# Opening of a two-layer diffusion step in two halves of the features, and its keys and values stored as soon as they are complete

## The chip, the core and the metric

The kernel runs on one core of one Trainium2 chip. Its engines are TensorE (PE in the profile, with PEld for the loading of weights), VectorE (DVE), ScalarE (ACT), GpSimd (POOL) and SyncE (SP); each runs its own stream of instructions in order, and they wait for each other on semaphores. Transfers are issued from the streams of SP, ACT and POOL. The metric is the device time in microseconds of one execution, median of several.

## What is computed

One inference step on 128 context tokens and 256 latent tokens (three tiles of 128 tokens, 1024 features, everything float32). Two layers, each a token mixer and then a mixture of experts; the first mixer is a gated linear recurrence (HGRN2), the second differential attention:

```python
for i in range(DEPTH):                                   # DEPTH = 2
    sh1, sc1, g1, sh2, sc2, g2 = split(silu(cond) @ w_ada[i] + b_ada[i], 6)
    h = rmsnorm(x, norm_g[i, 0]) * (1.0 + sc1) + sh1
    if i == 0:
        y, new_state = hgrn2_mixer(h, ...)               # q, inp, zf, zb, g = split(h @ w_in, 5)
    else:
        q, k, v = split(h @ w_qkv, 3); q, k = rmsnorm(q), rmsnorm(k)
        new_k, new_v = k, v                              # of the context tokens: outputs
        y = diff_attention(rotary(q), concat(rotary(k), cache_k), concat(v, cache_v)) @ w_out
    x = x + g1 * y
    h = rmsnorm(x, norm_g[i, 1]) * (1.0 + sc2) + sh2
    x = x + g2 * hier_moe(h, ...)                        # 16 experts, two for each token
```

`cond` is one vector for the context tokens and another for the latent ones. The shift `sh1` and the scale `sc1` have 1024 numbers each.

## The kernel before

Every engine's stream is written out by hand, in one function, `trunk`, with a block for each engine; nothing is scheduled by a tool. Weights stream from the chip's memory into a ring of eight slots of 2 MB (`ring`, `full`: it has landed, `used`: PE is done with it). SP issues them in the order in which its block names them, and waits for `used` before it fills a slot again.

**The opening.** `w_ada` comes in blocks of 512 columns, 2 MB each (`ada`). Blocks 0 and 1 are the shift, blocks 2 and 3 the scale; 0 and 2 belong to features 0 to 511 (k = 0 to 3 of eight groups of 128), 1 and 3 to features 512 to 1023 (k = 4 to 7). SP issues block 0, the tokens `x`, blocks 1 to 3, then the weights of head 0 (`head(0, 4, 0)`, four transfers of 512 KB), the masks and the states, head 1, and so on. On PE a block goes through 8 products with `cT` (`modulation_products`), ACT copies the result out of PSUM to `raw` (`raw_out`), PE turns it (`turn_rows`, 4 transposes), and DVE sums it into `adaln` (`block_columns`). When all four blocks are in, DVE makes `mod` (`columns`), and ACT and DVE write the modulated tokens `uT` (12 instructions each, `modulate`) from the tiles that PE has transposed before (`turn_tile`, 8 transposes for a tile). Then PE projects head 0: `proj(0, 0, 0, part)` for part 0 to 8. Parts 0, 2 and 4 are the products of q, zf and zb with features k = 0 to 3, parts 1, 3 and 5 those with k = 4 to 7 (4 products of 128x384 each), parts 6 to 8 the values (24 products of 128x128). Then `scan(0, ...)` starts; during the scan of one head PE projects the next. In the profile a product in float32 shows as two MATMUL records, so x8 there is 4 products.

**Keys and values.** In the second layer PE makes 18 products of `w_qkv` (b = 0 to 17: 0 to 5 queries, 6 to 11 keys, 12 to 17 values; b = 6 and 9 are the context keys, normalised into `AT["kp"]`, which lies in `xn[:, 1]`; b = 12 and 15 are the context values in `AT["v"][:, 0]`). ACT copies each out. After all 18 it issues the two stores `out["new_v"]` and `out["new_k"]`, 512 KB each, both counted by `at["out"]`. The attention then runs over 24 units (head, tile): for unit u PE makes the scores, DVE takes their maxima (`maxima`), ACT the exponentials, DVE the difference (`difference`), PE transposes and multiplies with the values, DVE writes the result into `xn[:, t]` (`attended`, u = 1 writes into tile 1, where the keys lie). Before the first maxima, DVE waits until both stores have landed:

```python
            dve.wait_ge(at["out"], 32)
            dve.wait_ge(at["ckT_ready"], 2)
            maxima(0)
```

In the attention PE also makes one block of the second layer's `w_ada` for every three units (`late_product`, 8 products, in line between the units), and the expert weights' slots come free as blocks, attention and output products end. Both expert stages stream 100 MB each through the ring.

Of the kernel before, what the change touches and what calls it, by code (L numbers as in the profile page):

```python
# [129 lines left out]
def trunk(nc, a, out):  # L130
    with ExitStack() as ctx:
# [45 lines left out]
        def down_rows(slot):  # L177
# [19 lines left out]
            mod_cols=("mod_cols", 0, 12), mod_ready=("mod_ready", 0, 2), diag=("diag", 0, 8),  # L197
# [40 lines left out]
        EARLY = 4  # L238

# [115 lines left out]
        def _(sp):  # L355
# [53 lines left out]
            ada(0, 0, 0, 0)  # L409
            sp.dma_start(x_rows[:, 0, :], a["x_prompt"][0]).then_inc(x_in, 16)  # L410
            sp.dma_start(x_rows[:, 1:3, :], a["x_sample"][0].rearrange("(t p) d -> p t d", p=P)).then_inc(x_in, 16)
            for blk in range(1, 4):
                ada(0, blk, blk, 0)
            head(0, 4, 0)
            sp.dma_start(masks[:, :, :].rearrange("p n t -> p (n t)"), a["const_mask"]).then_inc(heads_in, 16)
# [40 lines left out]
        def _(pe):  # L456
# [25 lines left out]
            def first_modulation(raw):  # L482

                ada_block(0, 0, 0)
                ada_block(1, 0, 1)
                first_turn(0, raw)
                need(pe, 0, "xn_ready", 1)
                turn_tile(0, "xT_done", xn, 0, (4, 5))
                ada_block(2, 0, 2)
                first_turn(1, raw)  # L490
                need(pe, 0, "xn_ready", 2)
                turn_tile(0, "xT_done", xn, 1, (0, 1))
                ada_block(3, 0, 3)
                first_turn(2, raw)
                first_turn(3, raw)
                need(pe, 0, "xn_ready", 3)
                turn_tile(0, "xT_done", xn, 2, (2, 3))

            def first_turn(blk, raw):
                if blk >= 2:  # L500
                    need(pe, 0, "mod_cols", blk - 1)
                turn_mod(0, blk, raw, blk % 2, 6 + blk % 2, blk + 1)
# [239 lines left out]
            first_modulation(raw)  # L742
# [112 lines left out]

            need(pe, 0, "uT_act", T)
            need(pe, 0, "uT_dve", T)
            for part in range(9):
                proj(0, 0, 0, part)
# [168 lines left out]
        def _(act):  # L1028
# [56 lines left out]
            def second_norm_end(n):  # L1085

                need(act, n, "mod_ready", 2)
# [74 lines left out]
            for blk in range(4):  # L1162
                raw_out(0, HG["raw"], blk % 2, blk, blk, 1, blk - 1 if blk >= 2 else None)
            need(act, 0, "mod_ready", 1)
            for t, src in enumerate((4, 0, 2)):
                modulate(0, "xT_done", "uT_act", t, src)
# [88 lines left out]
            need(act, 1, "mod_ready", 1)  # L1255
# [5 lines left out]
            for b in range(18):  # L1261
                act.wait_ge(at["proj"], b + 1)
                if b < 12:

                    if b >= 2:
                        act.wait_ge(at["turned"], b - 1)
                    A(AT["sq"][:, b % 2, :], bank[b % 2][:, :], ACT.Square).then_inc(at["squares"], 1)
                    act.wait_ge(at["meansq"], b + 1)
                    A(stat[:, 2, 0:8], stat[:, 1, 0:8], ACT.Sqrt).then_inc(at["root"], 1)
                else:  # L1270
                    half, t = divmod(b - 12, T)
                    A(AT["v"][:, t, 512 * half:512 * half + 512], bank[b % 2][:, :], ACT.Copy).then_inc(at["v_ready"], 1)
# [71 lines left out]
        def _(dve):  # L1344
# [29 lines left out]
            def columns(n, norm, first_part, blocks):  # L1374
# [5 lines left out]
                    .then_inc(S[n]["mod_ready"], 1)  # L1380
# [283 lines left out]
            for blk in range(4):  # L1664
                block_columns(0, blk, 6 + blk % 2, blk + 1)
            columns(0, 0, 0, 4)
            need(dve, 0, "mod_ready", 1)
            for t, src in enumerate((5, 1, 3)):
                modulate(0, "xT_done", "uT_dve", t, src)
# [114 lines left out]
            need(dve, 0, "mod_ready", 2)  # L1784
# [7 lines left out]
            columns(1, 0, 0, 4)  # L1792
# [6 lines left out]
            need(dve, 1, "mod_ready", 1)  # L1799
# [223 lines left out]
```

## Time and profile before

| | us |
|---|---|
| median of 3 runs | 1255.93 (1255.23 to 1256.7) |
| the profiled execution, its own time | 1257.95 |
| its span in the trace | 1256.1 |
| PE busy | 1122.5 (89% of the span) |
| DVE, ACT, POOL busy | 427.5, 226.4, 135.8 |
| moved by DMA | 317.08 MB, mean 252 GB/s |

The profiled execution is 2.02 us above the median of the runs, and 1.85 us longer than its span. All times of rows count from the start of the span.

### The profile page before, as it was taken

Reading aid. Unit: us, or ns where it says so; the run is one execution under the profiler, and the core shown is the slowest. Engines: PE = TensorE matmul, PEld = TensorE weight load, DVE = VectorE, ACT = ScalarE, POOL = GpSimd, SP = SyncE. Lnnn points to the kernel's source line nnn. Section 1 sums busy time; section 2 is a strip of 40 time slices with the busy share of each in tenths; the row PEclk is TensorE's granted clock in tenths of the full one; section 3 lists DMA queues with packets and bytes.
Section 4 is the critical chain, followed back from the end, with each engine's and each line's share of the span. In section 5 each row is a group of like instructions: output and inputs, shape, how many; then the busy total and the mean of one; then the engine's idle time right before and its main releaser. Section 6 shows DMA issues by size and latency. Waiting matters only on the chain.

```text
span 1256.1 us, 19811 instructions
## 1 busy us (share of the span) xinstructions
PE 1122.5 (89%) x8500; PEld 673.4 (54%) x8500; DVE 427.5 (34%) x1102; ACT 226.4 (18%) x527; POOL 135.8 (11%) x219
## 2 busy tenths in 40 slices
PE   4899999998899989999986799987989799999894
PEld 1566666665444566666653344434545656666551
DVE  1155555555522350000003755306853330000006
ACT  2201010111121321111000311115632211101010
POOL 0334333333100000000002100000000000000012
PEclk8899999999899989999998899998999699999897
DMA  9974444434923338999999913135761169999993
GB/s 347 272 237 135 136 136 135 135 135 160 373 109 129 134 132 325 427 424 425 424 426 409 342 67 134 67 133 199 262 244 67 69 268 403 426 425 425 426 423 151
DMA packets 97601, 317.08 MB, mean 252 GB/s; under 512 B 3792, under 2 KB 38912, under 8 KB 81120
## 3 DMA queue, kind: packets, MB, share of 16 engines
q1 hardware_dynamic: 90160, 298.05, 62.0%
q10 hardware_dynamic: 5248, 10.97, 2.2%
q0 software_dynamic: 2096, 6.67, 1.5%
q8 instruction: 72, 1.18, 0.4%
q14 instruction: 25, 0.20, 0.0%
HBM read 304.67 MB, written 11.01 MB: 251 GB/s over the span
## 4 chain that ended last, share of the span: by engine, by line
issue 70%; PE 20%; DMA 3%; DVE 3%; SPq 2%; POOL 1%; ACT 0%; POOLq 0%; DVEq 0%
PE bank L757 11%; PE bank L766 4%; DMA ring<-expert_rows,moe_row 2%; PE bank L782 2%; PE bank L468 1%; SPq L360 1%; SPq L372 1%; DVE ring L1632 1%; DMA ring<-in_w_ada 1%; DMA ring<-in_hgrn_w_in 1%; PE bank L838 1%; PE bank L791 0%; DVE hg_kf L1714 0%; DVE uT L1630 0%; PE bank L831 0%
## 5 line engine op out<-in xcount | busy, mean ns | idle before, releaser
L656 PE MATMUL bank<-ring,xn 128*64 128x256 f32 x1536 | 174.0, 384 | 12.0 <-DMA ring<-in_moe_w_up 7.9
L656 PEld LDWEIGHTS bank<-ring,xn 128*64 128x64 f32 x1536 | 110.8, 139 | 77.8 <-issue 11.2
L757 PE MATMUL bank<-uT,ring 128*128 128x384 f32 x384 | 137.6, 504 | 4.5 <-DMA ring<-in_hgrn_w_in 4.5
L945 PE MATMUL bank<-ring,uT 128*128 128x512 f32 x288 | 126.3, 593 | 1.3 <-issue 1.3
L1620 DVE TENSOR_TENSOR moe_hh<-xn,bank 128x256 f32<-128x256 f32 x32 | 13.5, 421 | 307.7 <-ACT xn L1125 307.6
L670 PE MATMUL bank<-ring,xn 128*64 128x512 f32 x384 | 88.4, 614 | 15.5 <-DMA ring<-in_moe_w_down 15.5
L645 PE MATMUL bank<-moe_g,moe_h 128*128 128x128 f32 x768 | 96.6, 285 | 2.4 <-DVE moe_g L1518 2.4
L645 PEld LDWEIGHTS bank<-moe_g,moe_h 128*128 128x128 f32 x768 | 92.6, 200 | 7.9 <-issue 7.9
L757 PEld LDWEIGHTS bank<-uT,ring 128*128 128x128 f32 x384 | 70.9, 193 | 47.1 <-ACT uT L1048 4.7
L1973 POOL TENSOR_TENSOR moe_flag<-con 128x1 f32<-128x1 f32 x2 | 0.4, 192 | 862.3 <-DMA expert_rows<-xn 862.3
L945 PEld LDWEIGHTS bank<-ring,uT 128*128 128x128 f32 x288 | 53.6, 190 | 65.1 <-issue 65.1
L574 PE MATMUL bank<-ring,uT 128*128 128x512 f32 x192 | 84.0, 593 | 0.8 <-ACT uT L1068 0.8
L670 PEld LDWEIGHTS bank<-ring,xn 128*64 128x64 f32 x384 | 28.7, 142 | 66.4 <-issue 65.4
L468 PE MATMUL bank<-ring,cT 128*32 128x512 f32 x384 | 53.2, 677 | 8.6 <-DMA ring<-in_w_ada 8.6
L1675 DVE COPY_PREDICATED hg_att<-masks,bank 128x384 f32<-128x384 uint8 x104 | 59.9, 576 | 0.0
L574 PEld LDWEIGHTS bank<-ring,uT 128*128 128x128 f32 x192 | 35.9, 190 | 43.0 <-issue 42.1
L656 PE MATMUL bank<-moe_ring,xn 128*64 128x256 f32 x512 | 57.2, 380 | 0.2 <-DMA moe_ring<-in_moe_w_up 0.2
L1125 ACT ACTIVATE xn<-bank 128x256 f32<-128x256 f32 x32 | 12.3, 383 | 205.2 <-PE bank L656 205.2
L656 PEld LDWEIGHTS bank<-moe_ring,xn 128*64 128x64 f32 x512 | 38.3, 137 | 20.1 <-issue 3.9
L766 PE MATMUL bank<-ring,uT 128*128 128x128 f32 x384 | 47.2, 277 | 0.0
L766 PEld LDWEIGHTS bank<-ring,uT 128*128 128x128 f32 x384 | 44.7, 192 | 0.6
L879 PE MATMUL bank<-ring,uT 128*128 128x512 f32 x96 | 42.2, 594 | 0.6 <-DVE adaln L1370 0.5
(261 smaller groups left out, 1262.7 us busy)
## 6 DMA issues: line engine op xcount, KB each, us to landing
ring<-in_w_ada SPq DMA_DIRECT2D x24, 2048.0 KB, 9.8
ring<-in_moe_w_gate SPq DMA_DIRECT2D x24, 2048.0 KB, 18.1
ring<-in_moe_w_up SPq DMA_DIRECT2D x24, 2048.0 KB, 22.3
ring<-in_moe_w_down SPq DMA_DIRECT2D x24, 2048.0 KB, 27.5
ring<-in_hgrn_w_in SPq DMA_DIRECT2D x32, 512.0 KB, 8.2
moe_ring<-in_moe_w_gate SPq DMA_DIRECT2D x8, 2048.0 KB, 22.5
moe_ring<-in_moe_w_up SPq DMA_DIRECT2D x8, 2048.0 KB, 24.2
moe_ring<-in_moe_w_down SPq DMA_DIRECT2D x8, 2048.0 KB, 21.2
```

The costliest lines, as they stand in the source:

```text
L468: last = mm(bank[to][32 * g:32 * g + 32, :], cT[:, 2 * g + r, :], cols(slot)[:, 2 * g + r, :], start=(r == 0), stop=(r == 1))
L574: last = mm(bank[4 + half][:, :], uT[:, k, t * P:(t + 1) * P], cols(slot)[:, k, :], start=(k == 0), stop=(k == KC - 1))
L645: last = mm(bank[half][:, k * P:(k + 1) * P], m["h"][:, t, (4 * half + k) * P:(4 * half + k + 1) * P], m["g"][:, t, :, :], start=(t == 0), ...
L656: last = mm(bank[2 + e][64 * g:64 * g + 64, 256 * part:256 * part + 256], m["xe"][:, k, 64 * e:64 * e + 64], cols(slot)[:, k, 256 * g:256 ...
L670: last = mm(bank[5 + 2 * half][64 * e:64 * e + 64, :], m["hT"][:, e, j, 64 * g:64 * g + 64], rows_of[e][:, g, j, 512 * half:512 * half + 512],
L757: last = mm(to[:, 0:TOK], w[:, k, f, :], uT[:, k, :], start=(k == 0), stop=(k == KC - 1))
L766: last = mm(bank[3][:, t * P:(t + 1) * P], uT[:, k, t * P:(t + 1) * P], w[:, k, 1, :], start=(k == 0), stop=(k == KC - 1))
L782: last = mm(to[g * size:(g + 1) * size, here], lhs[:, here], rhs[:, here], start=True, stop=True)
L879: last = mm(bank[4 + half][:, :], uT[:, k, t * P:(t + 1) * P], cols(2 + half)[:, k, :], start=(k == 0), stop=(k == KC - 1))
L945: last = mm(bank[b % 2][:, :], uT[:, k, t * P:(t + 1) * P], cols(slot)[:, k, :], start=(k == 0), stop=(k == KC - 1))
L1620: v.tensor_tensor(m["hh"][:, e, :], m["sg"][:, e, :], bank[2 + e][:, 256:512], ALU.mult)\
L1675: return v.copy_predicated(HG["att"][:, :].rearrange("p (t n) -> p t n", t=T), mask, src[:, 0:TOK].rearrange("p (t n) -> p t n", t=T))
```

## The change

Two independent places are changed.

First the opening. SP issues `x` first, then the blocks in the order 0, 2, head 0, 1, 3. PE, ACT and DVE finish the first half of the features (blocks 0 and 2, k = 0 to 3 of all three tiles) before the second. A block's products all go to bank 6 and its transposes to bank 7, so that a block waits for the copy of the one before (`mod_raw`). The transposes of `x` go by halves as well, into banks 3 to 5, those of the second half once the first half has been read. ACT modulates tile 0 and DVE tiles 1 and 2 of each half. PE makes parts 0 and 2 of head 0 with the first half of `uT`, then the blocks 1 and 3, then part 4, and the other six parts once the second half of `uT` is there. Counts of `mod_ready` go up by one everywhere behind it.

Second the stores. ACT issues `new_k` in the turn of b = 10 and `new_v` in that of b = 16; DVE waits for their landing not before the first maxima but before `attended(1)`.

```diff
+        FIRST_BLOCKS = (0, 2, 1, 3)
...
-            ada(0, 0, 0, 0)
             sp.dma_start(x_rows[:, 0, :], a["x_prompt"][0]).then_inc(x_in, 16)
             sp.dma_start(x_rows[:, 1:3, :], a["x_sample"][0].rearrange("(t p) d -> p t d", p=P)).then_inc(x_in, 16)
-            for blk in range(1, 4):
-                ada(0, blk, blk, 0)
+            ada(0, 0, 0, 0)
+            ada(0, 2, 2, 0)
             head(0, 4, 0)
+            ada(0, 1, 1, 0)
+            ada(0, 3, 3, 0)
...
+            def first_block(at, raw):
+
+                if at >= 1:
+                    need(pe, 0, "mod_raw", at)
+                ada_block(FIRST_BLOCKS[at], 0, 6)
+
+            def first_turn(at, raw):
+
+                if at >= 1:
+                    need(pe, 0, "mod_cols", at)
+                turn_mod(0, None, raw, at % 2, 7, at + 1)
+
+            def first_features(half):
+
+                for t in range(T):
+                    need(pe, 0, "xn_ready", t + 1)
+                    for j in range(4):
+                        k = 4 * half + j
+                        last = nc.tensor.transpose(bank[3 + t][:, j * P:(j + 1) * P], xn[:, t, k * P:(k + 1) * P], ident)
+                    last.then_inc(S[0]["xT_done"], 1)
...
-            first_modulation(raw)
+            first_block(0, raw)
+            first_turn(0, raw)
+            first_block(1, raw)
+            first_features(0)
+            first_turn(1, raw)
+            need(pe, 0, "uT_act", 1)
+            need(pe, 0, "uT_dve", 1)
+            first_features(1)
...
+            proj(0, 0, 0, 0)
+            proj(0, 0, 0, 2)
+            first_block(2, raw)
+            first_turn(2, raw)
+            first_block(3, raw)
+            first_turn(3, raw)
+            proj(0, 0, 0, 4)
             need(pe, 0, "uT_act", T)
             need(pe, 0, "uT_dve", T)
-            for part in range(9):
+            for part in (1, 3, 5, 6, 7, 8):
                 proj(0, 0, 0, part)
...
+                if b == 16:
+                    act.wait_ge(at["v_ready"], 4)
+                    act.dma_start(out["new_v"][0, 0].rearrange("p h d -> p (h d)"), AT["v"][:, 0, :]).then_inc(at["out"], 16)
...
-            act.wait_ge(at["v_ready"], 6)
-            act.dma_start(out["new_v"][0, 0].rearrange("p h d -> p (h d)"), AT["v"][:, 0, :]).then_inc(at["out"], 16)
-            act.dma_start(out["new_k"][0, 0].rearrange("p h c d -> p (h c d)"),
-                          AT["kp"][:, :, :].rearrange("p b n -> p (b n)")).then_inc(at["out"], 16)
+                if b == 10:
+                    act.wait_ge(at["normed"], 10)
+                    act.dma_start(out["new_k"][0, 0].rearrange("p h c d -> p (h c d)"),
+                                  AT["kp"][:, :, :].rearrange("p b n -> p (b n)")).then_inc(at["out"], 16)
...
-            dve.wait_ge(at["out"], 32)
             dve.wait_ge(at["ckT_ready"], 2)
             maxima(0)
             for u in range(len(units)):
                 if u + 1 < len(units):
                     maxima(u + 1)
                 difference(u)
+                if u == 2:
+                    dve.wait_ge(at["out"], 32)
                 if u >= 1:
                     attended(u - 1)
```

On PE, in the opening before (`bank<-ring,cT` are the products of a block of w_ada, `bank<-con,hg_raw` its transposes, `bank<-con,xn` the transposes of the tokens, `bank<-uT,ring` the projections):

```order
L468 MATMUL bank<-ring,cT 32x512 x16
L474 MATMUL bank<-con,hg_raw 128x128 x4
L560 MATMUL bank<-con,xn 128x128 x8
L468 MATMUL bank<-ring,cT 32x512 x8
L474 MATMUL bank<-con,hg_raw 128x128 x4
L560 MATMUL bank<-con,xn 128x128 x8
L468 MATMUL bank<-ring,cT 32x512 x8
L474 MATMUL bank<-con,hg_raw 128x128 x8
L560 MATMUL bank<-con,xn 128x128 x8
L757 MATMUL bank<-uT,ring 128x384 x24
L766 MATMUL bank<-ring,uT 128x128 x24
L773 MATMUL bank<-hg_q,hg_kd 128x128 x6
```

And the same place on PE after the change:

```order
L470 MATMUL bank<-ring,cT 32x512 x8
L476 MATMUL bank<-con,hg_raw 128x128 x4
L470 MATMUL bank<-ring,cT 32x512 x8
L502 MATMUL bank<-con,xn 128x128 x12
L476 MATMUL bank<-con,hg_raw 128x128 x4
L502 MATMUL bank<-con,xn 128x128 x12
L765 MATMUL bank<-uT,ring 128x384 x8
L470 MATMUL bank<-ring,cT 32x512 x8
L476 MATMUL bank<-con,hg_raw 128x128 x4
L470 MATMUL bank<-ring,cT 32x512 x8
L476 MATMUL bank<-con,hg_raw 128x128 x4
L765 MATMUL bank<-uT,ring 128x384 x16
```

The instructions are the same in number; two of the four blocks, and their transposes, now stand between the first 8 and the other 16 products of the projection, and no block stands back to back with another any more.

On ACT, at the end of the 18 products of the second layer, before (`xn<-bank` and `stat<-stat` stand for the norm of b = 10 and 11, `at_kT<-bank` for the turned keys, `at_v<-bank` for the copies of b = 12 to 17):

```order
L1267 ACTIVATE xn<-bank 128x512
L1269 ACTIVATE stat<-stat 128x8
L1279 ACTIVATE at_kT<-bank 128x4x128
L1272 ACTIVATE at_v<-bank 128x512
L1279 ACTIVATE at_kT<-bank 128x4x128
L1272 ACTIVATE at_v<-bank 128x512 x5
L1282 DMA out_new_v<-at_v 128x1024
L1283 DMA out_new_k<-xn 128x1024
L1287 ACTIVATE at_kT<-bank 128x4x128 x2
L1290 ACT_TABLE_LOAD
```

and after:

```order
L1306 DMA out_new_k<-xn 128x1024
L1287 ACTIVATE xn<-bank 128x512
L1289 ACTIVATE stat<-stat 128x8
L1302 ACTIVATE at_kT<-bank 128x4x128
L1292 ACTIVATE at_v<-bank 128x512
L1302 ACTIVATE at_kT<-bank 128x4x128
L1292 ACTIVATE at_v<-bank 128x512 x4
L1295 DMA out_new_v<-at_v 128x1024
L1292 ACTIVATE at_v<-bank 128x512
L1310 ACTIVATE at_kT<-bank 128x4x128 x2
L1313 ACT_TABLE_LOAD
```

The store of the values now stands ahead of the last copy, and that of the keys nine instructions above it; the copies of the cached keys no longer have a store ahead of them.

## Rows read from the trace of the kernel before

**Rows 1.** The page: the span

```profile
span 1256.1 us, 19811 instructions
```

**Rows 2.** The chain that ended last, opening: start us, us, what

```profile
30.90 8.70 DMA ring<-in_hgrn_w_in
...
58.52 5.36 PE bank L766 x48
...
78.37 2.78 PE bank L757 x8
```

**Rows 3.** Timeline of the opening: start us, us, engine, line, operation [idle before <-releaser]

```profile
11.08 3.64 PE L468 MATMUL bank<-ring,cT 128*32 128x512 f32 x16 [0.27 <-DMA ring<-in_w_ada]
...
14.81 1.06 ACT L1033 ACTIVATE xn<-x 128x1024 f32<-128x1024 f32 x1 [9.12 <-DMA x<-in_x_sample]
...
20.25 3.64 PE L468 MATMUL bank<-ring,cT 128*32 128x512 f32 x16 [5.52 <-DMA ring<-in_w_ada]
...
23.82 1.11 PE L474 MATMUL bank<-con,hg_raw 128*128 128x128 f32 x4
...
25.99 1.92 PE L468 MATMUL bank<-ring,cT 128*32 128x512 f32 x16
...
28.34 1.04 PE L560 MATMUL bank<-con,xn 128*128 128x128 f32 x8
...
31.14 1.92 PE L468 MATMUL bank<-ring,cT 128*32 128x512 f32 x16 [1.76 <-DMA ring<-in_w_ada]
...
33.87 0.63 PE L474 MATMUL bank<-con,hg_raw 128*128 128x128 f32 x4 [0.22 <-ACT hg_raw L1057]
...
34.53 0.19 DVE L1369 TENSOR_REDUCE adaln<-bank 128x8 f32<-128x32 f32 x1 [0.46 <-PE bank L474]
...
35.25 3.92 DVE L1397 TENSOR_SCALAR uT<-bank,mod 128x128 f32<-128x128 f32 x12
...
39.85 18.67 PE L757 MATMUL bank<-uT,ring 128*128 128x384 f32 x48 [4.48 <-DMA ring<-in_hgrn_w_in]
```

**Rows 4.** Windows: us, busy of PE, PEld, DVE, ACT, POOL, PEclk, DMA share, GB/s

```profile
40.00:45.00 5.00, 5.00 (x8) 2.68 (x9) 0.00 (x0) 0.00 (x0) 0.00 (x0) 0.50 1.05 204
...
848.00:853.00 5.00, 0.00 (x0) 0.00 (x0) 1.35 (x5) 0.66 (x4) 0.00 (x0) 0.50 0.49 194
853.00:858.00 5.00, 4.80 (x21) 1.27 (x21) 3.13 (x11) 1.65 (x7) 0.00 (x0) 0.50 0.00 0
859.00:862.00 3.00, 2.75 (x19) 1.97 (x20) 1.92 (x7) 2.73 (x12) 0.00 (x0) 1.00 0.57 185
```

**Rows 5.** Waits from 830 to 870 us: engine, line, for whom: us, times, longest

```profile
DVE stat L1855 <- DMA out_new_k<-xn: 6.3, 1, 6.3
```

**Rows 6.** Timeline of the end of the projections and the first attention units

```profile
833.89 0.60 ACT L1272 ACTIVATE at_v<-bank 128x512 f32<-128x512 f32 x1 [6.27 <-PE bank L945]
...
841.39 0.35 ACTq L1282 DMA_DIRECT2D out_new_v<-at_v  x1
...
841.77 0.45 ACTq L1283 DMA_DIRECT2D out_new_k<-xn  x1
842.27 1.09 ACT L1287 ACTIVATE at_kT<-bank 128x512 f32<-128x512 f32 x2 [0.91 <-PE bank L958]
...
843.41 1.14 PE L973 MATMUL bank<-at_kT,at_qT 64*128 64x128 f32 x8 [0.90 <-ACT at_kT L1287]
...
845.17 0.15 DVE L1847 TENSOR_SCALAR lam<-lam 128x1 f32<-128x1 f32 x1
851.61 0.49 DVE L1855 TENSOR_REDUCE stat<-bank 128x1 f32<-128x128 f32 x2 [6.29 <-DMA out_new_k<-xn]
...
853.20 1.65 PE L973 MATMUL bank<-at_kT,at_qT 64*128 64x384 f32 x4 [8.65 <-ACT uT L1315]
...
855.19 3.38 PE L468 MATMUL bank<-ring,cT 128*32 128x512 f32 x16
```

**Rows 7.** DMA issues from 700 to 960 us: KB each, us to landing

```profile
out_new_v<-at_v ACTq DMA_DIRECT2D x1, 512.0 KB, 8.9
```

More of the change, by code:

```diff
@@ L196, in trunk @@
             mod_raw=("mod_raw", 0, 12), mod_T=("mod_T", 0, 12),
-            mod_cols=("mod_cols", 0, 12), mod_ready=("mod_ready", 0, 2), diag=("diag", 0, 8),
+            mod_cols=("mod_cols", 0, 12), mod_ready=("mod_ready", 0, 3), diag=("diag", 0, 8),
             gate_mm=("gate_mm", 0, 8), gate_ready=("gate_ready", 0, 8), out_mm=("out_mm", 0, 6),
@@ L480, in turn_mod @@
                 turn_rows(raw, b, to).then_inc(S[n]["mod_T"], 1)
[L482 to L502, printed above, removed]
+            def first_block(at, raw):
[13 more added lines that the diff above has]
+                    last.then_inc(S[0]["xT_done"], 1)
             def early_product(blk):
@@ L1085, in second_norm_end @@
             def second_norm_end(n):
-                need(act, n, "mod_ready", 2)
+                need(act, n, "mod_ready", 3)
                 modulate(n, "xT2_done", "uT2_act", 0, 0)
@@ L1161, in _ @@
                 root(0, "mean_ready", "root", t)
[L1162 to L1166, printed above, removed]
+            for half in range(2):
+                for at_block in (2 * half, 2 * half + 1):
+                    raw_out(0, HG["raw"], at_block % 2, 6, FIRST_BLOCKS[at_block], 1, at_block - 1 if at_block >= 2 else None)
+                need(act, 0, "mod_ready", half + 1)
+                need(act, 0, "xT_done", T * half + 1)
+                for j in range(4):
+                    k = 4 * half + j
+                    last = A(uT[:, k, 0:P], bank[3][:, j * P:(j + 1) * P], ACT.Identity,
+                             bias=mod[:, 0, k, 0:1], scale=mod[:, 1, k, 0:1])
+                last.then_inc(S[0]["uT_act"], half + 1)
             def head_out(h, b, heads_done):
@@ L1254, in _ @@
             root(1, "mean_ready", "root", 2)
-            need(act, 1, "mod_ready", 1)
+            need(act, 1, "mod_ready", 2)
             for t, src in enumerate((6, 2, 5)):
@@ L1372, in _, with columns @@
             parts = [adaln[:, n, :, :, :].rearrange("p (a b) j c -> p a (b j) c", b=2) for n in range(2)]
-            def columns(n, norm, first_part, blocks):
+            def columns(n, norm, first_part, blocks, steps=1):
                 need(dve, n, "mod_cols", blocks)
@@ L1379, in columns @@
                 v.scalar_tensor_tensor(mod[:, 1, :, :], parts[n][:, first_part + 1, :, :], 1.0, g, ALU.add, ALU.mult)\
-                    .then_inc(S[n]["mod_ready"], 1)
+                    .then_inc(S[n]["mod_ready"], steps)
             def gate_diagonal(n, raw, part, which, q):
@@ L1663, in _ @@
                 normalise(0, "root", "xn_ready", t)
[L1664 to L1669, printed above, removed]
+            for half in range(2):
+                for at_block in (2 * half, 2 * half + 1):
+                    block_columns(0, FIRST_BLOCKS[at_block], 7, at_block + 1)
+                here = slice(4 * half, 4 * half + 4)
+                need(dve, 0, "mod_cols", 2 * half + 2)
+                v.tensor_copy(mod[:, 0, here, :], parts[0][:, 0, here, :])
+                v.scalar_tensor_tensor(mod[:, 1, here, :], parts[0][:, 1, here, :], 1.0,
+                                       small[:, here].unsqueeze(2).broadcast_to([P, 4, 2]), ALU.add, ALU.mult)\
+                    .then_inc(S[0]["mod_ready"], 1)
+                need(dve, 0, "mod_ready", half + 1)
+                need(dve, 0, "xT_done", T * half + T)
+                for t in (1, 2):
+                    for j in range(4):
+                        k = 4 * half + j
+                        last = v.tensor_scalar(uT[:, k, t * P:(t + 1) * P], bank[3 + t][:, j * P:(j + 1) * P],
+                                               mod[:, 1, k, 1:2], mod[:, 0, k, 1:2], ALU.mult, ALU.add)
+                last.then_inc(S[0]["uT_dve"], half + 1)
             dve.wait_ge(heads_in, 32)
@@ L1783, in _ @@
             update_x(0, HG["sg"], 1, 1)
-            need(dve, 0, "mod_ready", 2)
+            need(dve, 0, "mod_ready", 3)
             modulate(0, "xT2_done", "uT2_dve", 0, 1)
@@ L1789, in _ @@
             own = Chain(dve, own_dve[1])
-            columns(1, 0, 0, 4)
+            columns(1, 0, 0, 4, 2)
             mean(1, "squares", "mean_ready", 0)
@@ L1798, in _ @@
             normalise(1, "root", "xn_ready", 2)
-            need(dve, 1, "mod_ready", 1)
+            need(dve, 1, "mod_ready", 2)
             for t, src in enumerate((4, 3, 7)):
```

## The prediction, made before the changed kernel was run

> **What bounds the kernel now.** I read the page first, then the chain of work that ended last, then the timelines and waits of the two places that the change touches, and the granted clock last. The span is 1256.1 us [rows 1]; the sum below is made against the profiled execution's own 1257.95 us, and 2.02 us are then taken off, since the median of the runs is 1255.93. PE is busy for 89% of the span, so a gain can only come from a hole in PE's work or from PE running at the higher clock; both places hold such a hole.
>
> The opening is a race between the loads and PE. Block 0 is used from 11.08, `x` is in at 14.81, block 1 at 20.25 and block 3 at 31.14, so two blocks take 10.9 us and one 5.4 [rows 3]. Head 0, of the same size, comes 8.70 us later, and PE, idle for 4.48 us, starts on it at 39.85 [rows 2, 3]. From there PE does not wait: the projections take 18.67 us, the values 5.36 from 58.52, and the scan of head 0 can start at 63.88 [rows 2, 3]. That is the number to beat. Everything behind it up to the first experts hangs on PE and on slots that PE frees, so I take a shift of this point as carried whole.
>
> The second place is at 841 to 853 us. The stores are issued at 841.39 and 841.77; PE has the first scores from 843.41; DVE is done with its small work at 845.32 (845.17 + 0.15) and then stands until 851.61, 6.3 us, for the store of the keys; PE stands 8.65 us until 853.20 [rows 5, 6]. Nothing else is missing in this time: the inputs of the first maxima are there. The PE clock then runs at half until 858, and is back at 1.00 by 859 [rows 4].
>
> **The stores.** Removed is the wait of DVE. What is late next is DVE's own work before it, done at 845.32. So the first maxima move from 851.61 to about 845.35: 6.3 us. The two issues in ACT's stream (0.35 and 0.45 us) leave the place before the copies of the cached keys, which start at 842.27, just as the second issue ends, though PE's first transposes must be done a little before [rows 6]. I give this 0.1 us, between 0 (the copy was waiting for PE, as the row says) and 0.4. In their new places the issues cost nothing: before the change ACT waits 6.27 us for PE ahead of the copy of b = 16, which ends at 834.49 [rows 6], and the condition of each issue is the copy or the turn that ACT has just waited for. The wait itself moves to u = 2. The store of the values, issued at about 834.6, lands 8.9 us later [rows 7], at 843.5; DVE reaches the wait only when the third unit's difference is done, well after 850, so there it costs nothing. If that cover were gone, up to the old 6.3 us would come back.
>
> **The clock in the attention.** After the hole of 8.65 us the first block of 8 products takes 3.38 us, where it takes 1.92 at the full clock, and the third scores 1.65 [rows 3, 6]. The half clock thus costs about 1.5 us on PE in a stretch where PE, ACT and DVE wait for each other, and perhaps 0.5 more. After the change PE's hole is 8.65 - 6.3 = 2.4 us. The trace has the clock fall after the holes of 4.48 and 8.65 us, and the block behind the 1.76 us before 31.14 still runs at full rate, 1.92 [rows 3, 4, 6]. 2.4 us is nearer to the latter, but the scores before it are thin work. I take 0.7 us of gain, a third of what the half clock costs; the bounds are 2.0 (no fall) and -1.0 (it falls all the same, and then covers a microsecond more of work than now). The Trainium skill, "TensorE: Matmul & The Clock Gate", section "Why this matters for your kernels", says that an idle gap of some length between bursts sends TensorE back to half its clock and that shorter ones do not. By it the clock would stay up here, and this term would be 2.0 instead of 0.7; the row of 8.65 us agrees with its first half, and no row here has a hole of 2.4 us.
>
> **The opening.** I put the new order on the old durations [rows 2, 3].
> - Loads. `x` first: landed near 9.6 (14.81 less the 5.4 of a block). Block 0 is then in at 14.8, block 2 at 20.2, head 0 at 28.9 (8.70 more), block 1 at 34.3, block 3 at 39.7. The sum of bytes up to there is the same, so masks, states and head 1 come as before, but POOL's small loads, which start when slot 3 is full, start at 39.7 instead of 31.
> - First half. Products of block 0: 14.8 to 18.5 (3.64, the cold rate of both first blocks). Copy and turn: 0.8 + 1.11, to 20.4. Block 2 is in; it takes between 3.64 and 1.92, I say 2.7, since it starts cold and ends warm: 23.1. Transposes of half of `x`, 12 of them: three times 1.04 less two overlaps, 2.9: 26.0. Turn 0.63 at full rate: 26.6. DVE from the turn to the first scaling: 35.25 - 34.53 = 0.7, and 8 scalings at 3.92/12 = 0.33: 2.6. The first half of `uT` is there at 29.9.
> - PE cannot go on sooner, for the other 12 transposes go into the banks that DVE and ACT have just read. They take 2.9 warm; cold they take between that and the 1.11/0.63 of a cold turn, I say 3.9. PE has stood for 3.3 us, between the 1.76 and the 4.48 us above, and I take the clock as fallen: 33.8. Head 0 has been in for 5 us, so its load is hidden; what is late next is PE.
> - Parts 0 and 2: a part of 4 products (x8) takes 2.6 to 2.78 warm, and twice this cold, since 8 records fill the 5.00 us from 40 to 45 at a clock of 0.50 [rows 4]. One microsecond of cold work is left, 5.2 + 0.7: 39.7.
> - Blocks 1 and 3, which before lay partly under the loads and now stand in the middle: each 1.92, then 0.8 until its copy is out (31.14 + 1.92 = 33.06 to 33.87) and 0.63 to turn: 3.35 twice: 46.4. Block 3 is in at 39.7 and wanted at 43.0, so 3.3 us to spare.
> - Part 4, 2.6: 49.0. DVE needs 0.1 + 0.7 + 2.6 after the last turn: 49.8, so PE stands 0.8 us. Parts 1, 3, 5: 7.8, to 57.6. Values 5.36: 63.0.
>
> Against 63.88 this is 0.9 us sooner. Nearly all of the wait for head 0 that is removed comes back as work that was hidden under the loads: two blocks with their copies (6.7 us), 12 transposes, and the wait for the second half. With a clock that stays up at 29.9, it is 61.2 (2.7 us sooner); with a first half later by 1 us and a cold stretch of twice the length, 65.9 (2 us later). Head 1 and the masks are wanted at 63.0 and later, and land as before.
>
> **The sum.** 6.3 + 0.1 + 0.7 + 0.9 = 8.0 us. 1257.95 - 8.0 = 1249.95 for a profiled execution, less 2.02: 1247.9. I put 1248.2, since the places share the risk that a clock term is lost.
>
> **The rivals.** 0.2% is 2.5 us, about what a measurement of this kernel can tell from no change.
> 1. The forecast: the stores' wait gone, the opening nearly even. 1246.5 to 1250.5. Chance 0.54. For it: DVE's row names one releaser, and all other inputs are there.
> 2. The clock stays up in both places. Gains 6.4 + 2.0 + 2.7 = 11.1: 1244.8. For it: both holes are shorter than any after which a fall is seen. Against it: both come behind thin work. Chance 0.16.
> 3. The opening loses. The two blocks in the middle, each with its copy, and a longer cold stretch cost 2 us or more, and the attention's clock falls too: 6.4 + (-1.0) + (-2.0) = 3.4 gained, 1252.5; a little worse and it is within 0.2%. Chance 0.18, of which 0.03 beyond 1253.4.
> 4. The wait moves and is not removed: the store of the values lands only behind the third unit. It decides when it takes more than about 16 us instead of 8.9, for then it ends after 850.5. All of 6.3 is lost and with it the clock's 0.7; 1255.93 - 1.0 = 1254.9 is left: the change doesn't do what it says. Against it: the slot loads beside it at 840 are the only other traffic. Chance 0.05.
> 5. Slower: the loads behind head 0 come late. PE takes its blocks in order, so while it waits for block 3 it can do no part of head 0 that is ready. Block 3 is wanted at 43.0 and due at 39.7; head 1, wanted at 63.0, lands behind it. If rows of 512 B, which already make head 0 take 8.70 instead of 5.4, slow the queue with POOL's loads beside them so that block 3 or head 1 come d us behind their time, the end moves by d; to be slower by 0.2% it takes d = 8.0 + 2.5 = 10.5, which gives 1258.4. Chance 0.03. The other 0.04 I leave for what I have not seen, most of it between no change and the forecast.
>
> Faster: 0.54 + 0.16 + 0.15, and 0.02 of the last: 0.87. Same: 0.10. Slower: 0.03. The range reaches from rival 2's 1244.8 to rival 3's 1252.5; a little over 1 in 10 is left out above it and half of that below.
>
> **What the profile after would show.** Right: DVE's first maxima start 1 us or less behind its small work on `lam`, with no wait for a store there or at u = 2; PE's hole before the third scores is 2 to 3 us; `out_new_v` is issued some 7 us before the last product ends. In the opening the first projection starts at 33 to 34, the scan of head 0 at 61 to 65, PE stands 3.3 us before the second transposes and under 1 us before part 1, and never for head 0. The block in the attention takes 1.92 if the clock stays up, 3.4 if not. The prediction is wrong if PE waits for block 1, block 3 or head 1, if the scan starts after 66, or if DVE waits for a store at u = 2.

## The result, and the profile after

The changed kernel takes 1244.65 us, median of 5 runs (1243.3 to 1249.09), beside 1256.29 (1255.23 to 1256.7) for the kernel before in the same comparison. The ratio is 0.9912, with a 95% interval of 0.9898 to 0.9926: 11.1 us are gone (9.3 to 12.8). The forecast was 8 us, at 1248.2; the direction is right, the size too small, and the time stands at the low end of the range, 1244.8: just under it by the median, just above it by the ratio (0.9912 x 1255.93 = 1244.9). The profiled execution of after took 1244.65 us itself, 13.3 us less than that of before, so its times need no correction to the median.

The page of after, its first lines (beside [rows 1]):

```profile
span 1242.8 us, 19820 instructions
PE 1118.5 (90%) x8500; PEld 670.7 (54%) x8500; DVE 428.4 (34%) x1108; ACT 225.4 (18%) x523; POOL 136.2 (11%) x219
```

PE does the same 8500 instructions in 4.0 us less busy time (1122.5 before), so most of the 13.3 us are holes that closed. The timeline of PE, ACT and DVE in the opening of after (start us, us, engine, line, operation, idle before and its releaser), to be laid beside [rows 3]:

```profile
14.30 3.64 PE L470 MATMUL bank<-ring,cT 128*32 128x512 f32 x16 [3.81 <-DMA ring<-in_w_ada]
18.64 1.11 PE L476 MATMUL bank<-con,hg_raw 128*128 128x128 f32 x4 [0.71 <-ACT hg_raw L1072]
19.75 3.10 PE L470 MATMUL bank<-ring,cT 128*32 128x512 f32 x16
22.78 1.53 PE L502 MATMUL bank<-con,xn 128*128 128x128 f32 x12
24.15 0.60 PE L476 MATMUL bank<-con,hg_raw 128*128 128x128 f32 x4
...
25.49 2.64 DVE L1701 TENSOR_SCALAR uT<-bank,mod 128x128 f32<-128x128 f32 x8
...
28.23 2.07 PE L502 MATMUL bank<-con,xn 128*128 128x128 f32 x12 [3.48 <-issue]
30.10 6.48 PE L765 MATMUL bank<-uT,ring 128*128 128x384 f32 x16
36.51 1.92 PE L470 MATMUL bank<-ring,cT 128*32 128x512 f32 x16
...
42.99 2.75 PE L765 MATMUL bank<-uT,ring 128*128 128x384 f32 x8
46.69 7.98 PE L765 MATMUL bank<-uT,ring 128*128 128x384 f32 x24 [0.95 <-DVE uT L1701]
54.50 5.52 PE L774 MATMUL bank<-ring,uT 128*128 128x128 f32 x48
59.86 1.50 PE L781 MATMUL bank<-hg_q,hg_kd 128*128 128x128 f32 x12
```

PE waits for block 0 and for nothing else that is loaded. The 3.48 us that are put down to "issue" end when DVE has scaled its eight tiles (25.49 + 2.64 = 28.13): PE stands there for the banks that hold the first half. The last row is the scan of head 0, at 59.86; the same row of before starts at 63.72 in its trace (the prediction worked with 63.88, the end of the values). This is 3.9 us sooner. It is one execution of each: the traces of this opening start the scan at 58.21, 58.24, 58.79 and 59.86 us, and the five traces with the old opening at 63.27 to 63.96, which is 5.0 us by the means.

The timeline of after where the projections end and the attention begins, the counterpart of [rows 6]:

```profile
826.97 0.35 ACTq L1295 DMA_DIRECT2D out_new_v<-at_v  x1
...
835.17 1.09 ACT L1310 ACTIVATE at_kT<-bank 128x512 f32<-128x512 f32 x2 [0.74 <-PE bank L973]
...
836.31 1.14 PE L988 MATMUL bank<-at_kT,at_qT 64*128 64x128 f32 x8 [0.74 <-ACT at_kT L1310]
...
838.07 0.15 DVE L1881 TENSOR_SCALAR lam<-lam 128x1 f32<-128x1 f32 x1
838.26 0.49 DVE L1889 TENSOR_REDUCE stat<-bank 128x1 f32<-128x128 f32 x2
...
839.85 0.92 PE L988 MATMUL bank<-at_kT,at_qT 64*128 64x384 f32 x4 [2.39 <-ACT uT L1338]
...
841.10 3.42 PE L470 MATMUL bank<-ring,cT 128*32 128x512 f32 x16
```

DVE goes from its work on `lam` to the first maxima with 0.04 us between. PE's hole is 2.39 us instead of 8.65: 6.26 us less. The copies of the cached keys wait 0.74 us for PE's transposes instead of 0.91, which is what the two issues had cost. But the block still takes 3.42 us, as in [rows 6].

Where the 13.3 us of span lie, from the two traces: 3.9 us up to the scan of head 0; 4.0 more between it and the selection of the first experts (`moe_sel`, shown below, 444.55 before and 436.73 after); 6.3 in the attention's hole; and 0.8 given back in the rest.

### The profile page after: what moved, and what is told of

Same layout as the page of the kernel before. It is cut to its first block, busy times and chain, and to the rows that moved or that the text cites. A ratio compares the mean times of both kernels' runs of the same rounds, so it can differ in the third digit from the quotient of the medians.

```text
span 1242.8 us, 19820 instructions
## 1 busy us (share of the span) xinstructions
PE 1118.5 (90%) x8500; PEld 670.7 (54%) x8500; DVE 428.4 (34%) x1108; ACT 225.4 (18%) x523; POOL 136.2 (11%) x219
## 4 chain that ended last, share of the span: by engine, by line
issue 70%; PE 19%; DMA 3%; DVE 2%; POOL 1%; ACT 0%; POOLq 0%; DVEq 0%
PE bank L765 10%; PE bank L774 4%; DMA ring<-expert_rows,moe_row 2%; DMA ring<-in_w_ada 2%; PE bank L790 2%; PE bank L470 1%; DVE ring L1655 1%; PE bank L846 1%; PE bank L799 0%; PE bank L839 0%; DVE uT L1653 0%; PE bank L857 0%; DVE hg_kf L1748 0%; PE bank L476 0%; DVE uT L1665 0%
## 5 line engine op out<-in xcount | busy, mean ns | idle before, releaser
L1643 DVE TENSOR_TENSOR moe_hh<-xn,bank 128x256 f32<-128x256 f32 x32 | 13.5, 422 | 307.9 <-ACT xn L1140 307.8
```

What stands on the lines that cost most here:

```text
L1643: v.tensor_tensor(m["hh"][:, e, :], m["sg"][:, e, :], bank[2 + e][:, 256:512], ALU.mult)\
```

## The experiments

**One change at a time.** The first kernel is the changed one with the edits of the stores undone; the second is the kernel before with these edits alone:

```diff
+                if b == 16:
+                    act.wait_ge(at["v_ready"], 4)
+                    act.dma_start(out["new_v"][0, 0].rearrange("p h d -> p (h d)"), AT["v"][:, 0, :]).then_inc(at["out"], 16)
...
-            dve.wait_ge(at["out"], 32)
...
+                if u == 2:
+                    dve.wait_ge(at["out"], 32)
```

> The opening of the change alone, stores as before. The prediction's sum gave it 0.9 us; the trace of the changed kernel starts the scan of head 0 at 60.0 instead of 63.9. Theory A (the opening is worth its own shift, and the clock's half stretches near 310 to 335 us depend on where the shift puts PE's thin work): 3.9 us plus 0 to 3, so 1249.5 to 1252.5. Theory B (the opening is worth 0.9 us and the rest of the 11.6 us lies in the attention): 1255.4. Rival: the shift is lost in a later wait, 1256.3.

> The stores of the change alone, opening as before. Theory A: DVE's wait of 6.3 us goes, and a little of PE's cold stretch behind it: 6.3 to 8.0 us, so 1248.3 to 1250. Together with the opening alone it should add up to the 11.6 us of the change within 1.5 us. Rival (the two changes gain only together): under 5 us, above 1251.

Measured: opening alone 1251.76 us, ratio 0.9952 (0.9937 to 0.9966), 6.0 us gained; stores alone 1249.78, ratio 0.994 (0.9923 to 0.9958), 7.5 us gained. Both are as expected. The sum, 13.5, and the 11.1 of both together differ by less than their intervals allow for (some 3 us), so the two places add up as far as these runs can tell. The opening is worth several times the 0.9 us of the prediction. In its own trace the scan of head 0 starts at 58.24.

**The two halves of the stores' change.** The stores early, with DVE's wait left ahead of the first maxima:

```diff
+                if b == 16:
+                    act.wait_ge(at["v_ready"], 4)
+                    act.dma_start(out["new_v"][0, 0].rearrange("p h d -> p (h d)"), AT["v"][:, 0, :]).then_inc(at["out"], 16)
...
+                if b == 10:
+                    act.wait_ge(at["normed"], 10)
+                    act.dma_start(out["new_k"][0, 0].rearrange("p h c d -> p (h c d)"),
+                                  AT["kp"][:, :, :].rearrange("p b n -> p (b n)")).then_inc(at["out"], 16)
...
             dve.wait_ge(at["out"], 32)
             maxima(0)
```

> Before, with both stores issued early, but DVE still waits for their landing ahead of the first maxima. Theory A (what counts is that the store has landed): the value store lands some 9 us after 834, at 843.5, before DVE is ready at 845.3, so the whole gain of the stores stays: within 0.5 us of stores_only. Rival (the place of the wait counts): no gain, 1256.

And the wait moved, with the stores left at the end of the projections:

```diff
-            dve.wait_ge(at["out"], 32)
             maxima(0)
...
+                if u == 2:
+                    dve.wait_ge(at["out"], 32)
```

> Before, with DVE's wait moved to the third unit, stores issued where they were. The key store lands at 851.6; the wait is reached some 5 to 7 us after the first maxima at 845.3. Theory A: a part of the gain stays, 4 to 6 us, since DVE does the work of two units first and then waits about 1 us or nothing: 1250 to 1252. Rival: the stall only moves, under 1 us gained, above 1255.

Measured: 1250.7 us, ratio 0.9948 (0.993 to 0.9965), and 1250.1 us, ratio 0.9943 (0.9927 to 0.9959). Stores alone were 0.994. Each half does the whole, and the second adds nothing that these runs, with intervals of 2 us to either side, can tell. The second kernel was expected to keep only a part. In both traces PE's hole is 2.39 us. The timeline of the kernel with the moved wait:

```profile
842.71 0.35 SPq L406 DMA_DIRECT2D ring<-in_moe_w_up  x1
843.30 0.35 ACTq L1282 DMA_DIRECT2D out_new_v<-at_v  x1
...
843.69 0.45 ACTq L1283 DMA_DIRECT2D out_new_k<-xn  x1
...
847.08 0.15 DVE L1847 TENSOR_SCALAR lam<-lam 128x1 f32<-128x1 f32 x1
847.27 0.49 DVE L1855 TENSOR_REDUCE stat<-bank 128x1 f32<-128x128 f32 x2
```

The store of the keys is issued at 843.69 and lands 10.0 us later, by the DMA rows of this trace:

```profile
out_new_v<-at_v ACTq DMA_DIRECT2D x1, 512.0 KB, 9.1
out_new_k<-xn ACTq DMA_DIRECT2D x1, 512.0 KB, 10.0
```

It is thus under way until 853.7, behind the first maxima. DVE comes to its wait only when the third unit's difference is done, near 857.5 in this trace, and shows no wait for the store there. The same rows of the kernel with the early stores:

```profile
out_new_k<-xn ACTq DMA_DIRECT2D x1, 512.0 KB, 2.6
out_new_v<-at_v ACTq DMA_DIRECT2D x1, 512.0 KB, 3.0
```

The same 512 KB lands in a third of the time in the early place. In the late place SP fills a slot with `in_moe_w_up`, 2 MB, 0.59 us before, and the two stores are under way together. Which of the two slows them was not tested apart.

**The loads of the opening in the old order** (on PE, ACT and DVE everything as in the changed kernel):

```diff
+            ada(0, 0, 0, 0)
...
-            ada(0, 0, 0, 0)
-            ada(0, 2, 2, 0)
+            for blk in range(1, 4):
+                ada(0, blk, blk, 0)
             head(0, 4, 0)
-            ada(0, 1, 1, 0)
-            ada(0, 3, 3, 0)
```

> The changed kernel with SP's loads back in the order of before (block 0, x, blocks 1 to 3, head 0), PE's, ACT's and DVE's order as changed. Theory A (PE is bound by its own order once head 0 is in): head 0 lands near 39.8, and from the first projection to the scan of head 0 the changed order needs 29.9 us (30.1 to 60.0 in its trace), so the scan starts near 69.7 and the time is that of the changed kernel plus 9.7: 1254.6. Rival (the new order of work is better by itself, the loads matter little): under 1248.

Measured: 1255.77 us, ratio 0.9995 (0.9985 to 1.0005): nothing is left of the gain, about as expected. (The median is that of 11 executions. A twelfth took 2929 us and is left out of it and of the ratio; nothing on record explains it.) Its timeline of PE in the opening:

```profile
25.98 3.64 PE L469 MATMUL bank<-ring,cT 128*32 128x512 f32 x16 [4.38 <-DMA ring<-in_w_ada]
...
39.36 8.30 PE L764 MATMUL bank<-uT,ring 128*128 128x384 f32 x16 [0.61 <-DMA ring<-in_hgrn_w_in]
...
70.94 1.50 PE L780 MATMUL bank<-hg_q,hg_kd 128*128 128x128 f32 x12
```

Block 2 is third in the queue and comes at 25.98 instead of 19.75, head 0 is awaited again, and the scan starts at 70.94, 7.2 us later than before the change. The 7.2 us lost here and the 6.3 of the attention, whose hole is 2.40 us in this trace too, cancel. The order of the engines without the order of the loads is a loss.

**No projection ahead of the blocks 1 and 3:**

```diff
-            proj(0, 0, 0, 0)
-            proj(0, 0, 0, 2)
             first_block(2, raw)
             first_turn(2, raw)
             first_block(3, raw)
             first_turn(3, raw)
+            proj(0, 0, 0, 0)
+            proj(0, 0, 0, 2)
             proj(0, 0, 0, 4)
```

> The changed kernel with parts 0 and 2 of head 0 behind blocks 1 and 3. PE then stands until block 1 has landed near 34 and block 3 near 38.5, and projects from 42: scan at 42 + 7.8 + 7.9 + 5.5 = 63.2 instead of 60.0, so Theory A says 3.2 us slower than the changed kernel, about 1248. Rival (the early parts only shift work about): within 1 us of the changed kernel, 1244 to 1246.

Measured: 1248.29 us, ratio 0.9931 (0.9917 to 0.9944), 2.4 us more than the changed kernel by the ratios and 3.6 by the medians. Its timeline of PE:

```profile
28.51 1.50 PE L502 MATMUL bank<-con,xn 128*128 128x128 f32 x12 [3.48 <-issue]
31.98 1.92 PE L470 MATMUL bank<-ring,cT 128*32 128x512 f32 x16 [1.97 <-DMA ring<-in_w_ada]
...
37.40 3.35 PE L470 MATMUL bank<-ring,cT 128*32 128x512 f32 x16 [2.06 <-DMA ring<-in_w_ada]
...
62.86 1.50 PE L781 MATMUL bank<-hg_q,hg_kd 128*128 128x128 f32 x12
```

PE now waits for both loads, 1.97 and 2.06 us, and the scan starts 3.0 us later than in after, 0.9 us sooner than before the change. The two parts that PE does early are what fills the wait for blocks 1 and 3. The full gain of the opening needs both: loads in the new order, and projections between them.

**What the half clock costs.** Products that serve nothing (448 columns of a constant) fill PE's hole before the third scores, so that PE's clock stays up; the rest is left as it is. Three of them in the changed kernel, 11 in the kernel before:

```diff
+            def filler(count, to):
+                for _ in range(count):
+                    mm(bank[to][:, 0:448], ones, con[:, 0:448], start=True, stop=True)
...
             scores(0)
             scores(1)
+            filler(3, 4)
```

> The changed kernel with three extra products of 128x448 (results not used) in PE's hole of 2.4 us at the start of the attention, to keep the clock up. The block behind it took 3.42 us at the half clock and takes 1.92 at the full one. Theory C (the clock's fall costs what the block is longer by): 1.5 to 2 us faster than the changed kernel. Rival (PE's time there is hidden behind DVE and ACT): no difference beyond 0.5 us. If the clock falls all the same, nothing is learnt but that such work doesn't hold it.

> The kernel before with eleven extra products of 128x448 (results not used, about 8.2 us at the full clock) in PE's hole of 8.65 us before the third scores. DVE's wait for the store stays, so only the clock changes. Theory C: 1.5 to 2.2 us faster than before, 1254 to 1255, with the block at 1.92 us instead of 3.38. Rival: no difference, 1256.

Measured: changed 1243.24 us, ratio 0.9884 (0.987 to 0.9898), 1.4 us under the changed kernel by the medians and 3.5 by the ratios, of intervals that just meet. Before 1255.53, ratio 0.998 (0.9967 to 0.9993), so 2.5 us (0.9 to 4.1). Expected were 1.5 to 2 us and 1.5 to 2.2. PE in the changed kernel with the fillers:

```profile
838.98 2.52 PE L741 MATMUL bank<-con 128*128 128x448 f32 x6
841.45 0.92 PE L993 MATMUL bank<-at_kT,at_qT 64*128 64x384 f32 x4
...
842.70 1.92 PE L470 MATMUL bank<-ring,cT 128*32 128x512 f32 x16
```

and in the kernel before with them:

```profile
853.39 1.92 PE L468 MATMUL bank<-ring,cT 128*32 128x512 f32 x16
```

The block takes 1.92 us in both: with work in the hole the clock does not fall there. What follows in after, and then in the changed kernel with the fillers (the last products with the values, and the first products behind the attention):

```profile
905.36 0.94 PE L1008 MATMUL bank<-at_v,uT 128*128 128x128 f32 x6 [0.58 <-ACT uT L1321]
907.76 1.12 PE L554 MATMUL bank<-at_mod,con 128*128 128x512 f32 x2 [1.47 <-DVE at_mod L1410]
```

```profile
905.47 0.94 PE L1013 MATMUL bank<-at_v,uT 128*128 128x128 f32 x6 [0.58 <-ACT uT L1327]
907.87 2.07 PE L554 MATMUL bank<-at_mod,con 128*128 128x512 f32 x2 [1.47 <-DVE at_mod L1416]
```

From the third scores to the last products with the values the changed kernel needs 65.5 us and with the fillers 64.0. The kernel before needs 66.2 and with the fillers 64.0. So the attention gets 1.5 and 2.2 us shorter. But the clock then falls right behind it (2.07 us where 1.12 stood), and up to the selection of the second layer's experts 1.0 and 1.5 us are given back, which leaves 0.4 and 0.7 us in these traces.

The same in the opening: two fillers ahead of block 0, four ahead of the second transposes; and then both places together.

```diff
             pe.wait_ge(c_steps, 2)
+            filler(2, 0)
...
             first_turn(1, raw)
+            filler(4, 0)
             need(pe, 0, "uT_act", 1)
```

> The changed kernel with two extra products of 128x448 before block 0 and four in the hole of 3.5 us before the second transposes (results not used). Theory: PE is cold for block 0 (3.64 us instead of 1.92) and for most of block 2 (3.10) and for a stretch from 29 us on; with the clock up the scan of head 0 starts at 57 to 58.5 instead of 59.9, 1.5 to 3 us faster in all. Rival (the loads bind as soon as PE is faster: block 2 lands no sooner than 19.5): 0.5 to 1.2 us. Second rival: extra work that cold doesn't warm PE, no change.

> The changed kernel with the extra products in the opening and in the hole of 2.4 us at the start of the attention. The attention's share was 0.4 us between profiles and 1.4 in the medians. If the two add: 2 to 4 us faster than the changed kernel, 1241 to 1243; if the clock only falls at another place instead, 1243 to 1245.

Measured: opening 1246.65 us, ratio 0.9925 (0.9912 to 0.9939), no gain where 0.5 to 3 us were expected; both 1242.97, ratio 0.9894 (0.9875 to 0.9912). PE with the opening's fillers:

```profile
13.71 2.10 PE L470 MATMUL bank<-ring,cT 128*32 128x512 f32 x16 [0.45 <-DMA ring<-in_w_ada]
...
19.29 1.92 PE L470 MATMUL bank<-ring,cT 128*32 128x512 f32 x16 [2.10 <-DMA ring<-in_w_ada]
...
27.93 5.33 PE L772 MATMUL bank<-uT,ring 128*128 128x384 f32 x16
...
38.80 3.20 PE L470 MATMUL bank<-ring,cT 128*32 128x512 f32 x16 [2.26 <-DMA ring<-in_w_ada]
...
60.14 1.50 PE L788 MATMUL bank<-hg_q,hg_kd 128*128 128x128 f32 x12
```

The first block takes 2.10 instead of 3.64, the first two parts 5.33 instead of 6.48, and all of it is lost again to waits for blocks 2 and 3; the scan does not start sooner. In the trace with both places filled PE waits 2.35 us for block 2 and not for block 3, and the scan starts at 58.89, no sooner than in the changed kernel either. With PE at the full rate the loads are the bound. So a faster PE in the opening brings nothing, and filling the attention's hole brings 1 to 4 us by the runs. Part of that spread may be whether the saved 1.5 us are given back: in the trace with both places filled the clock does not fall right behind the attention (1.12 us), and from the third scores to the selection of the experts it takes 135.8 us instead of 140.5. The lowest times measured are 1243.24 and 1242.97, which the runs do not tell apart.

**The changed kernel once more**, to see how its trace varies from execution to execution:

> The changed kernel once more, profiled anew. Theory D: of the 13.3 us between the two profiles, 10.1 are fixed (scan of head 0 sooner by 3.9, PE's hole at the attention shorter by 6.3) and some 3 come from where the half-clock stretches fell in those two executions (16.4 us of half clock before PE's hole at 441 us in the one, 4.5 in the other). Then the new profile has the same 3.9 +- 1 and 6.3 +- 0.1, while the stretch from 318 to PE's hole at 433 us may last anything from 114.9 to 118. Rival: that stretch is shortened by the change itself, and is again 114.9 +- 0.5.

Measured: 1244.77 us, ratio 0.9909 (0.9894 to 0.9925). The hole in the attention is 2.39 us again. The scan of head 0 starts at 58.21, which is 5.5 us sooner than before and more than the 3.9 +- 1 expected. The stretch behind it, up to the first experts, takes as long as in after (377.1 and 376.9 us), which is what the rival said. But the same code took 379.9 us in the kernel with the attention's fillers, so it is not fixed by the change.

## Why the prediction was right, and where too small

**The stores: right, to the tenth.** 6.3 us predicted, 6.26 measured, and 0.17 for the issues where 0.1 stood. The kernel with the stores alone gains 7.5 us (5.3 to 9.7), and the 6.4 of the sum lies within that. DVE waited for nothing in its place or at u = 2. Rival 4, that the wait only moves, is refuted by the kernel with the wait moved and the stores late: even a store that lands at 853.7 stands in nobody's way. What the prediction didn't see is that either half of the edit would have done, and that the 8.9 us from issue to landing belong to the old place: in the new one it is 2.6 to 3.0 us.

**The opening: the mechanism right, the term mis-sized.** 0.9 us predicted, 3.9 measured in the profiled execution (5.5 in the executions of the opening alone and of the second look at the changed kernel, where block 0 had landed 0.5 us sooner). By the prediction's own steps against the rows above: the turn of block 0 was over at 19.75 (20.4 predicted); block 2 took 3.0 us (2.7); the first 12 transposes 1.4 us until the turn (2.9); turn and DVE 4.0 (3.9); the second transposes 1.9 (3.9); parts 0 and 2 6.4 (5.9); blocks 1 and 3 with their copies 6.5 (6.7); part 4 and the wait 3.7 (3.4); the rest 13.2 (13.2). All but two are within 0.7 us. The step that failed is "12 of them: three times 1.04 less two overlaps, 2.9", and the 3.9 cold that rests on it, together 3.5 us too long. The row L560 x8 with 1.04 us [rows 3] was read as four transposes, as the note on products in float32 (two records each) suggests. But a transpose leaves one record: `turn_tile` makes 8 of them, and 8 records stand in the row. Twelve take 1.53 us. With this the sum would have been 11.5 instead of 8.0, and the forecast 1244.4. That this meets the measured time so closely is in part luck: in the other executions of this opening the scan starts 1.1 to 1.7 us sooner than in after.

**PE's clock in the opening: about as predicted.** PE stood for 3.48 us (3.3 predicted), and the clock had fallen behind it. The windows of after (us, busy of PE, PEld, DVE, ACT, POOL, PEclk, DMA share, GB/s), behind the opening's hole and behind the attention's:

```profile
28.00:33.00 5.00, 4.77 (x18) 3.57 (x19) 0.13 (x1) 0.00 (x0) 0.00 (x0) 0.66 1.05 387
...
841.00:845.00 4.00, 4.00 (x21) 1.04 (x20) 1.91 (x6) 0.95 (x4) 0.00 (x0) 0.57 0.00 0
```

A PEclk of 0.66 and 0.57 is a mixture of the chip's two levels, 1.2 and 2.4 GHz. Parts 0 and 2 took 6.48 us where the warm kernel needed 5.33, so 1.2 us; "One microsecond of cold work" stood in the prediction.

**The clock in the attention: the number right, the mechanism wrong.** 0.7 us of gain was taken, between 2.0 if the clock stays up and -1.0 if it falls, because a hole of 2.4 us seemed nearer to the harmless 1.76 than to 4.48. The hole came out at 2.39 us and the clock fell all the same (PEclk 0.57, the block 3.42 us). The Trainium skill, "TensorE: Matmul & The Clock Gate", section "Why this matters for your kernels", would have it stay up, as only a long gap sends the engine back; this case's rows disagree, and with them that part of rival 2 (1244.8) is refuted as a mechanism, though its number is the one that came out. A gain of 0.6 us is there even so, from the third scores to the last products with the values (66.2 us before, 65.5 in after): the clock fell later, so that the third scores take 0.92 us instead of 1.65. It is given back behind the attention, where the way to the selection of the experts takes 75.0 us instead of 74.3. That the term came out near 0.7 is luck. What the half clock costs in the attention itself is 1.5 us in the changed kernel and 2.2 before, by the kernels with fillers; the 2.0 of the prediction was a good estimate of the latter.

**What the prediction did not have: 4.0 us between the scan of head 0 and the first experts.** It took this stretch as shifted whole. From the row of the scan to this one it took 380.83 us before; in after 376.87:

```profile
436.73 0.69 PE L627 MATMUL bank<-moe_sel,con 128*128 128x64 f32 x2 [3.88 <-DVE moe_sel L1519]
```

PE does the same there; what differs between these two is how much of the work around the last scan runs at half clock. The windows of before and of after over the same work, then that of the changed kernel with fillers in the attention, whose program is the same up to 838 us:

```profile
300.00:340.00 40.00, 31.18 (x452) 17.48 (x445) 22.73 (x58) 5.46 (x8) 11.64 (x23) 0.83 0.96 357
```

```profile
296.00:336.00 40.00, 31.14 (x464) 16.11 (x457) 26.39 (x62) 5.46 (x8) 12.08 (x23) 0.96 0.99 372
```

```profile
296.00:336.00 40.00, 32.14 (x448) 17.42 (x441) 23.66 (x58) 5.46 (x8) 11.06 (x22) 0.83 0.97 359
```

At 0.83 some 14 us of the 40 run at half clock (40 x 0.17 x 2), at 0.96 some 3. From scan to `moe_sel` the third kernel needs 379.9 us, though its opening is the new one (scan at 58.79); the opening alone and the second look at the changed kernel need 377.1. But this place is not the only one. The kernel with the stores alone runs the same 40 us at 1.00 and still needs 380.3 us. Its clock falls sooner ahead of the experts: in the 20 us up to the row of `moe_sel` it is 0.68, and 0.88 in after. Its windows around the last scan and around the selection:

```profile
296.00:336.00 40.00, 28.59 (x480) 16.71 (x479) 22.72 (x62) 5.47 (x8) 12.35 (x23) 1.00 0.91 327
425.00:450.00 25.00, 17.53 (x83) 14.61 (x82) 10.06 (x48) 8.20 (x14) 0.00 (x0) 0.63 0.23 85
```

And with both places filled the stretch takes 380.9 us, though the clock over the last scan is 0.96 as in after: there PE stands for 2.5 us in three places for which the profile names no cause. Over all thirteen traces this stretch goes from 376.9 to 381.0, with every value under 379 in a kernel with the new opening, but with one execution of the same code at 379.9. So it moves by 3 us between executions of the same code, mostly through the clock. Whether the new opening makes the good case more frequent is open: three of its four executions have it, and none of the five with the old opening. The gain does not rest on it: the scan of head 0 came 3.9 to 5.5 us sooner and PE's hole in the attention is 6.3 shorter, in all traces of the changed kernel, which is 10.2 to 11.8 us beside the 11.1 of the ratio.

**The other rivals.** Rival 3, that the opening loses, is refuted: it gains 4 to 6 us alone. Its mechanism is real, but it needs late loads, as the run with the old order shows. Rival 5, that the loads behind head 0 come late, did not happen, but the margin was thinner than predicted. Block 3 was due at 39.7 and wanted at 43.0; it was in by 38.99, where POOL, which waits for it, issues its first small load:

```profile
38.99 1.09 POOL L1989 DMA_DIRECT2D wr<-in_moe_w_group  x1 [38.53 <-DMA ring<-in_w_ada]
```

PE wanted it at 39.80, so 0.8 us were to spare, not 3.3, since PE came to it 3.2 us sooner than predicted.

## What to carry to other kernels

Before a row's time is divided by a number of operations, count in the code how many it should hold: the count of records differs between kinds of operation in the same row format, and here it made a term of 4 us into one of 1. Where work is cut in halves to start earlier, the order of the loads is as much of the change as the order of the engines: here the one without the other lost 7 us, or kept about 1 of the 4 to 6 us. And where a wait for a transfer is the only thing that stands in the way, look first whether the wait can go behind work that does not need it: that was enough here, with the transfer as slow as ever.

## What the hardware showed that was not expected

- PE's clock falls behind short holes too. The block behind a wait of 2.39 us took 3.42, behind 2.26 us 3.20, behind 2.06 us 3.35; but behind 2.10 and 1.97 us it took 1.92. The length of the hole alone does not sort them.
- A store of 512 KB takes 2.6 to 3.0 us from issue to landing in the early place, and 8.9 to 10.0 us where SP issued a load of 2 MB 0.6 us before the first of two such stores.
- PE's first block takes 3.64 us behind the wait for its load, and 2.10 with four records of filler ahead of it.
- The same program differs by 3 us from execution to execution in one stretch of 380 us, mostly through where the granted clock falls (PEclk 0.96 or 0.83 over 40 us).
- Keeping the clock up in one place can make it fall in the next: with fillers in the attention's hole the products right behind the attention took 2.07 us instead of 1.12.
